# Gate 1's modulation parts made in the memory stage and kept in the bias rows; hybrid scores in a row, exponentials tile by tile

## The reference, cut to what matters

```python
c_act = jax.nn.silu(c)
mod = c_act @ w_ada[l] + b_ada[l]
sh1, sc1, g1, sh2, sc2, g2 = [m[:, None, :] for m in jnp.split(mod, 6, axis=-1)]
h = rms_norm_2(x, norm1_g[l]) * (1 + sc1) + sh1
proj = h @ w_in[l]
ca, cb, q, k, v, gate_conv, gate_attn = jnp.split(proj, offsets, axis=-1)
y_conv = conformer_conv(ca, cb, ...)          # conv, layer norm, silu, @ w_pw2 + b_pw2
y_attn = diff_attention(q, k, v, ...)         # 8 heads x 2 maps, softmax(map0) - lam*softmax(map1)
merged = jax.nn.sigmoid(gate_conv) * y_conv + jax.nn.sigmoid(gate_attn) * y_attn
x = x + g1 * (merged @ w_out[l])
...
x = x + g2 * moe_ffn(h2, ...)
```

## Time and profile before

| | |
|---|---|
| median of 3 runs | 1688.07 us (1686.02 to 1689.14) |
| the profiled execution | 1686.85 us |
| its span, first to last instruction | 1685.1 us |
| PE busy | 1578.4 us, 94% of the span |
| DVE / ACT busy | 712.1 us (42%) / 451.9 us (27%) |
| mean granted TensorE clock | 0.971 |
| memory stage | from about 446 to 584 us of the span |
| hybrid stage | from about 796 to 1097 us |

### The profile page before, as it was taken

The page is one execution under the profiler, slowest core; times in us unless marked ns, Lnnn a source line. Parts: engine busy times, 40 slices in busy tenths (PEclk is TensorE's granted clock), DMA queues, the critical chain, the costliest instruction groups (busy, mean ns, idle before and its releaser), DMA issues.

```text
span 1685.1 us, 26269 instructions
## 1 busy us (share of the span) xinstructions
PE 1578.4 (94%) x10058; PEld 1056.1 (63%) x10058; DVE 712.1 (42%) x1232; ACT 451.9 (27%) x729; POOL 44.1 (3%) x96
## 2 busy tenths in 40 slices
PE   6999989999998899998999989978998999999997
PEld 6999878668666499996854444554444444444443
DVE  4555346355213355554499754461121221212212
ACT  4333333141101243334001261022221222222221
POOL 5000000100000000000100000000000000000000
PEclk9999979999999999998999999979999999999999
DMA  9755473311331736446444462319997896988984
GB/s 317 268 174 175 150 252 113 125 51 51 128 135 65 251 128 206 161 163 238 167 150 150 150 225 75 134 54 358 340 389 293 326 362 211 338 326 294 343 324 167
DMA packets 154788, 350.78 MB, mean 208 GB/s; under 512 B 11615, under 2 KB 56879, under 8 KB 154160
## 3 DMA queue, kind: packets, MB, share of 16 engines
q1 hardware_dynamic: 151440, 342.98, 56.7%
q0 software_dynamic: 1792, 3.09, 0.7%
q10 hardware_dynamic: 1440, 3.17, 0.5%
HBM read 579.83 MB, written 2.16 MB: 345 GB/s over the span
## 4 chain that ended last, share of the span: by engine, by line
PE 44%; DVE 9%; DMA 6%; ACT 3%; SPq 3%; issue 2%; DVEq 0%; ACTq 0%
PE bank L2688 9%; PE bank L664 8%; PE bank L1963 6%; PE bank L2714 6%; DVE arena L2169 6%; PE bank L644 4%; PE bank L2621 3%; DMA ring<-in_w_exp_down 3%; DMA ring<-in_w_exp_gu 2%; PE bank L1954 2%; PE bank L484 2%; SPq L2937 2%; PE bank L2600 2%; ACT xn L2905 1%; PE bank L2580 1%
## 5 line engine op out<-in xcount | busy, mean ns | idle before, releaser
L664 PE MATMUL bank<-x_high,w_high 128*128 128x256 f32 x704 | 200.9, 285 | 6.1 <-DVEq L251 6.1
L664 PE MATMUL bank<-x_low,w_high 128*128 128x256 f32 x704 | 200.5, 285 | 0.0
L664 PE MATMUL bank<-x_high,w_low 128*128 128x256 f32 x704 | 199.5, 283 | 0.0
L1963 PE MATMUL bank<-ring,xT 128*128 128x512 f32 x384 | 168.3, 598 | 11.2 <-ACT arena L2326 11.2
L736 DVE TENSOR_TENSOR w_low<-ring,w_high 128x2048 fp32r<-128x2048 f32 x60 | 137.4, 2292 | 77.2 <-ACT w_high L701 77.2
L664 PEld LDWEIGHTS bank<-x_high,w_high 128*128 128x128 f32 x704 | 133.9, 190 | 7.6 <-issue 6.9
L1963 PEld LDWEIGHTS bank<-ring,xT 128*128 128x128 f32 x384 | 73.2, 192 | 102.5 <-issue 102.5
L664 PEld LDWEIGHTS bank<-x_high,w_low 128*128 128x128 f32 x704 | 135.2, 192 | 0.0
L664 PEld LDWEIGHTS bank<-x_low,w_high 128*128 128x128 f32 x704 | 134.2, 191 | 0.7
L2714 PE MATMUL bank<-ring,arena 128*32 128x512 f32 x1024 | 119.4, 607 | 14.9 <-DMA ring<-in_w_exp_down 7.1
L701 ACT ACTIVATE w_high<-ring 128x2048 fp32r<-128x2048 f32 x60 | 114.5, 1912 | 61.8 <-PE bank L644 59.2
(11 more groups left out here) (523 smaller groups left out, 2297.5 us busy)
## 6 DMA issues: line engine op xcount, KB each, us to landing
ring<-in_w_exp_gu SPq DMA_DIRECT2D x512, 512.0 KB
ring<-in_w_exp_down SPq DMA_DIRECT2D x128, 1024.0 KB
ring<-in_w_in SPq DMA_DIRECT2D x42, 768.0 KB, 5.8
ring<-in_ffn_w_gate SPq DMA_DIRECT2D x22, 1024.0 KB, 5.6
ring<-in_ffn_w_up SPq DMA_DIRECT2D x22, 1024.0 KB, 8.7
ring<-in_ffn_w_down SPq DMA_DIRECT2D x21, 1024.0 KB, 10.1
ring<-in_w_ada SPq DMA_DIRECT2D x24, 768.0 KB, 5.8
ring<-in_w_in SPq DMA_DIRECT2D x21, 512.0 KB, 6.8
```

The lines of the kernel that those rows point to most:

```text
L664: ins = pe.eng.matmul(bank[:, k * S:(k + 1) * S], ff_w[f][w][:, c, k, :], (x_high, x_low)[x][:, c, :], start=c == 0 and i == 0, stop=c == ...
L1963: ins = mm(ps[b][:], lhs[:, c, t * P:(t + 1) * P], w[:, c, :], start=c == 0, stop=c == DC - 1 and bias is None)
```

## The change

It has three parts.

- **Gate 1's parts move to the memory stage.** SP loads the two `w_ada` blocks between `mem_w_q` and `mem_w_o`. PE makes the first part after `last_values(1)`, the second after the softmax transposes; DVE copies both banks straight into `bias_rows`, which is no longer cleared. The bias rows are loaded into rows 1 to 7, beside the parts in rows 0, 32, 64, 96, so one column (`gate1_rows` = `group_heads` plus the column of `ident` that chooses the bias row) picks all five in a single matmul per bank.
- **Gate 1 is finished early**: its two banks come straight after the k features, and ACT copies them before the silu.
- **The hybrid's scores come in a row and the exponentials tile by tile**: PE makes `scores(0)`, the convolution's features, `scores(1)`, then both halves of the attention gate. DVE empties all score banks before it takes the first maximum. ACT puts the first half of the gate between `exps(0)` and `exps(1)`.

```diff
+    BIAS0 = ARENA - D
+    bias_rows, _ = carve(BIAS0, D)
+    gate1_rows = sb("gate1_row_heads", [P, 1])
...
     def memory():
         MH, HC = 4, 2
-        LEFT_OUT = 4
+        LEFT_OUT = 2
...
             release[mine] = (psum_full, pe.q.n)
+            gate_parts = pe_mod_parts(pe, psum_full, pe.q.fill)
+            next(gate_parts)
+            pe.released()
             for t in range(T):
                 pe.get()
...
                     ins.then_inc(psum_full, 1)
+            next(gate_parts)
+            pe.released()
             pe.get()
...
+            def gate1_part(n):
+                b = v.q.take()
+                do(e.tensor_copy(bias_rows[:, n * 512:(n + 1) * 512], ps[b][:]), psum_free)
+
+            gate1_part(0)
             for t in range(T):
                 for hd in range(0, MH, 2):
...
             v.feed()
+            gate1_part(1)
             take(oT, 4)
...
             for lo in (0, 512):
                 sp.project("mem_w_q", lo)
+            sp_mod(sp, GATE1)
             for lo in (0, 512):
                 sp.project("mem_w_o", lo, natural=True)
...
-            g(eng.memset(bias_rows, 0.0))
-            eng.dma_start(bias_rows[0:6], A["b_ada_2"].rearrange("l (j n) -> (l j) n", j=6))\
+            g(eng.tensor_tensor(gate1_rows[:], group_heads[:], ident[:, GATE1 + 1:GATE1 + 2],
+                                ALU.add))
+            eng.dma_start(bias_rows[1:7], A["b_ada_2"].rearrange("l (j n) -> (l j) n", j=6))\
                .then_inc(bias_loaded, 16)
...
-            wait(ln_ready, 1)
-            to_features(to_act, lambda t: convT[:, t])
+            wait(bias_loaded, 32)
+            for n in range(2):
+                b = to_act.fill()
+                mm(ps[b][:], gate1_rows[:].to_broadcast([P, P]),
+                   bias_rows[:, n * 512:(n + 1) * 512], start=True, stop=True)\
+                    .then_inc(act_full, 1)
             wait(qT_set, 1)
             wait(kT_set, 1)
             scores(0)
-            for _ in pe_mod_parts(pe, act_full, to_act.fill):
-                release.append((act_full, to_act.n))
-            w = wide[pe.slot()]
-            for t in range(T):
-                scores(1, slice(2 * t, 2 * t + 2))
-                tokens(to_act, w, xT, t)
-            release.append((act_full, to_act.n))
-            wait(parts_set, 2)
-            wait(bias_loaded, 32)
-            for n in range(2):
-                b = to_act.fill()
-                mm(ps[b][:], ident[:, GATE1:GATE1 + 1].to_broadcast([P, P]),
-                   bias_rows[:, n * 512:(n + 1) * 512], start=True, stop=False)
-                mm(ps[b][:], group_heads[:].to_broadcast([P, P]), gate_parts[:, n, :],
-                   start=False, stop=True).then_inc(act_full, 1)
+            wait(ln_ready, 1)
+            to_features(to_act, lambda t: convT[:, t])
+            scores(1)
+            projected(to_act)
             projected(to_act)
             soft_to_keys(0)
...
                     do(tt(dst[:, :, t * P:], got[:, :, t * P:], every(causal[:], len(maps)),
                           ALU.add), vec_free)
+            for t in range(T):
                 do(e.tensor_reduce(mx[:, t], tiles[t], AX.X, ALU.max))
...
             exps(0)
+            gates(gate_attn, 0)
             exps(1)
-            gates(gate_attn, 0)
-            for n in range(2):
-                b = mine.take()
-                evict(gate1[:, n * 512:(n + 1) * 512], ps[b][:])
-                a.eng.sem_inc(gate1_set, 1)
             gates(gate_attn, 1)
...
             for lo in (0, D, 512, D + 512, *range(2 * D, 6 * D, 512)):
                 sp.project("w_in_2", lo)
-            sp_mod(sp, GATE1)
             for lo in range(6 * D, 7 * D, 512):
                 sp.project("w_in_2", lo)
```

28 lines of the change are left out of this document (12 added, 16 removed).

## The result

The changed kernel took 1675.43 us (median of 4 runs) beside 1688.59 for the kernel before on the same chip: a ratio of 0.9931, with a 95% interval from 0.9912 to 0.9949. That is 11.7 us faster, between 8.6 and 14.9. Timed again with the experiments, the same kernel gave 1672.77 (6 runs), 0.9924 [0.9908, 0.9941]. The profiled execution's span is 1673.0 us, before 1685.1.

What follows compares the result with a forecast made beforehand. TensorE was taken as the bound, busy 94%, with 9.4 + 2.0 us that are no work at the hybrid's wait for ACT. Hybrid 11.4 gained minus memory stage 3.4 lost: 8.0 us faster, 1680.1, range 1675.5 to 1684.6.

Steps and rivals of the forecast that it cites:

- The hybrid: From the q and k features to soft_to_keys(0): PE's wait for ACT goes, 11.4 us gained, range 10 to 13.4.
- the sum: The forecast's step-by-step reckoning of the hybrid and memory stages: 11.4 gained less 3.4 lost, 8.0 us faster.
- took the fall: Hybrid: assumed PE's clock falls while half idle at 979 to 988, costing 2.0 us as at the old wait.
- The memory stage: Last values to product: PE waits for the second w_ada block until 546.8, 3.4 us lost, bounds 1.6 and 4.5.
- upper bound: Memory stage: half clock for both the second part and the product with the values, 4.5 us lost.
- Stage D's first cut: ACT's cut of stage D's first weight block moves from 556.81 to 568.0, and nobody is late.
- The fetch: Hybrid: issued at about 1024.7, lands in 8.1 us; up to 1.5 us of new wait in soft_to_keys(1), none taken.
- Both clocks up: The clock stays up in hybrid and memory stage: 11.8 us faster, 1676.3; chance 0.14.
- Slow scores: Hybrid: the slow clock hits scores(1), all behind 3.4 us later, 4.6 faster in all, 1683.5; chance 0.13.
- Even sharing of the queue: Memory stage: weight blocks served in turns, the second w_ada block in at 562.3; 7.5 us slower, 1695.6; chance 0.04.
- Gain taken back by the experts: Experts' transfers depend on the state of memory, not on when asked for: about 1687; chance 0.08.
- The wait only renamed: Hybrid: PE still waits before the gate's banks, nothing gained there; 3.4 us slower, 1691.5; no chance of its own.

Runs made afterwards that it cites:

- no_second_block: The change without loading or awaiting the second w_ada block, gate 1's second half made from the first (wrong values): 1667.11 us, ratio 0.9899, total not comparable.
- exps_in_row: The change with both sets of exponentials in a row and the attention gate's first half behind them: 1671.52 us, ratio 0.9908.
- part_behind: The change with gate 1's second part made behind the product with the values instead of ahead of it: 1673.75 us, ratio 0.9926.
- pw2_rows: The change with the second w_pw2 block read by rows like the w_in blocks (wrong row order in half the product): 1696.4 us, total not comparable.
- memory_only: The change with the hybrid back in its old order, gate 1's parts still made in the memory stage: 1687.72 us, ratio 1.0013 to the kernel before.
- before_again: The kernel before, unchanged, run once more for a second profile: 1683.92 us in one run.
- parts_in_wait: The kernel before with the hybrid's new order and one-matmul-per-bank gate 1, its parts staying in the hybrid: 1673.53 us, ratio 0.9923.

## Why the prediction was right, and what it missed

**The hybrid, right: 11.3 against 11.4, but two errors cancelled.** The wait for ACT went, and PE waited 4.8 us for DVE ("some 4 us"). The gate's tokens began 19.8 after the q and k features, where the sum had 17.7. Of these 2.1 us, 1.3 are the store, which the prediction took at its old landing of 979.9, and the other 0.8 are DVE's wait for the first pair of tile 1, which PE made at the half clock. On the other side it "took the fall" of the clock, for 2.0. The clock did fall, from about 984.4 to 987.8, the first row of the windows that stands at 0.50, but it was back at 1.00 before the tokens began, which took the 27.7 of the full clock. So the fall was placed right and priced wrong: it met some 3 us of scores instead of the gate, 0.8 on the path and not 2.0. That the store could land later was not in the sum at all. That the two errors cancel is luck.

**The memory stage, right: 3.0 against 3.4.** The second block arrived for PE at 546.99, forecast 546.8; the part took 3.17, between 1.8 and 3.6; the product 7.58. no_second_block shows that the cause is the named one. The sum's upper bound doesn't follow from its terms, though: with 3.6 for the part and the product's old 9.18 it is 546.8 + 3.6 + 9.18 = 559.6, 5.4 lost and not 4.5. Stage D's first cut came at 568.17, forecast 568.0, and held nobody up.

**The fetch, right.** It landed in 4.8 us instead of 8.1, and PE had no wait in `soft_to_keys(1)`, so the 1.5 kept for it were not needed. It was issued at 1028.32, 1.7 us later than the sum's 1024.7 (1.9 are added for the later start of the stage), since the exponentials began later; and `values(0)`, for which the sum saw no wait, waited 0.25. Its landing goes with its distance from the second `w_out` block. SP's queue, before, in the change and in exps_in_row:

```profile
1000.16 30.08 SPq L550 DMA_DIRECT2D ring<-in_w_out  x6
```
```profile
1005.69 15.16 SPq L550 DMA_DIRECT2D ring<-in_w_out  x6
```
```profile
1005.11 15.17 SPq L550 DMA_DIRECT2D ring<-in_w_out  x6
```

The fetch goes out 0.6 us behind the last of these issues in the kernel before and lands in 8.1, 3.6 behind in exps_in_row (6.0), 7.5 behind in the change (4.8). That agrees with the Trainium skill (DMA: Bandwidth & Descriptors, "Issuing engines are not separate DMA queues"), by which DMAs of SyncE and ScalarE interleave on the same engines.

**The step that failed is a sentence of the sum: "Stage D is TensorE's own work ... and the experts' weights can only be asked for after routing, so both just shift".** Stage D did shift (243.19 and 243.10). Two other stretches did not: the hybrid's first projections, which the sum doesn't name and so enters at nothing, and the experts.

- *The hybrid's first projections* took 1.5 us less. PE's timeline of before, of the change and of part_behind:

```profile
798.62 29.39 PE L1954 MATMUL bank<-xT,ring 128*128 128x256 f32 x128 [1.29 <-DVEq L251]
```
```profile
802.01 27.89 PE L1967 MATMUL bank<-xT,ring 128*128 128x256 f32 x128 [1.53 <-DVEq L251]
```
```profile
802.56 29.41 PE L1967 MATMUL bank<-xT,ring 128*128 128x256 f32 x128 [1.29 <-DVEq L251]
```

  The granted clock falls around PE's wait for the norm ahead of them. Windows of PE where it falls and where it is back (us, busy, clock, DMA share, GB/s), before and in the change:

```profile
790.62:791.62 1.00, 0.00 (x0) 0.91 1.05 389
...
801.62:802.62 1.00, 1.00 (x6) 0.97 1.05 385
```
```profile
796.01:797.01 1.00, 0.00 (x0) 0.84 1.05 403
...
800.01:801.01 1.00, 0.47 (x4) 0.95 1.06 389
```

  In the change it is back at about 800.1, before the projections start; in the kernel before it comes back at 801.7, 3 us into them. Over the thirteen profiles of the table there are just two values, 169.9 and 171.4 to 171.6. In the seven with the higher one the clock fell 2.3 to 2.8 us into the 4.5 us wait and stood at half for 10.2 us; in the six with the lower one, and in pw2_rows, it fell 4.0 to 5.1 us after the wait began, about where PE worked again, and stood at half for 3.4. The lower value is there where the memory stage's stretch was 22.6 or at least 26.7, the higher one where it was 23.8 to 25.8. The kernel part_behind makes the parts in the memory stage and has the higher value, so their place alone isn't the cause. Nor is it how late the stage begins: the projections began at 797.0 to 803.2 with the lower value, at 798.6 to 802.6 with the higher. What puts the fall at one place or the other, the runs don't settle.
- *The last stretch*, the experts, was 3.3 shorter, more than a quarter of the difference of the two profiles. The same code differs by 4.4 there from profile to profile, so one pair of traces can't tell it from chance. But it may not be chance alone: in the ten comparisons with four runs or more, pw2_rows and no_second_block left out, the measured difference (by the ratio) is 1.5 to 6.3 us lower than the sum of the six stretches ahead of the last one against the first profile of before, memory_only's among them (2.2 slower measured, 5.5 by the stretches). Against before_again, whose six are 1.4 longer, it is 0.1 to 4.9 lower. The last stretch is 532.8 on average in these ten profiles and 535.1 in the two of before. Whether that is a small gain by a mechanism, and which, stays open.

With these two left out, the stretches give 3.0 - 11.3 + 0.4, 7.9 faster, which is the forecast's 8.0; with the projections' 1.5 it is 9.4, inside the interval of the runs (8.6 to 14.9). The forecast gain was too small by 3.7 us (8.0 against 11.7). Everything outside the two stages was entered at zero, and the range held no gain that isn't in the edit: the projections' 1.5 are shown, and for the other 2.3 the last stretch is the likeliest place, which is not shown.

**The rivals.** Both clocks up: only in the gate's tokens. Slow scores: true for some 3 us of the scores, the first two pairs, and so for about 1 us of PE, not for all four pairs. Even sharing of the queue: no, the block was there at 546.99. Gain taken back by the experts: no sign. The wait only renamed: not in the change, but memory_only shows exactly this.

## What to carry to other kernels

Moving work out of a stage in which PE waits gives nothing: parts_in_wait, which leaves it in the wait, can't be told from the change, and memory_only, which only takes it out, is no faster than before. The order that lets the engine that empties banks go first is what pays; ask of each bank who empties it, and behind what. When work moves to an earlier stage, look at which ring slot its weights wait for: here the work itself was free and its load cost 4.3 us.

## What was not expected of the hardware

- The same stage has two lengths: the projections of the hybrid took 27.9 us in seven profiles and 29.4 to 29.7 in seven, for the same 128 instructions behind the same wait of 4.5 us, by whether the clock was back from its lower level before them or some 3 us into them.
- A store of 1 MB took 8.9 to 9.2 us beside one weight tensor's block and 10.2 to 10.5 beside another's of the same size, and not because of the pattern in which that block is read; a fetch of 1 MB took from 4.7 to 8.2 us, and the less the longer ago the last block of weights was issued (8.1, 6.0 and 4.8 at 0.6, 3.6 and 7.5 us).
- The last 530 us of the program vary by up to 4.4 us between two executions of the same code. The stretch from the start to the last values, ahead of the table, varies more: 526.5 us in memory_only's profile and 531.0 to 533.0 in five others with the same code up to there.
